# One streaming buffer for weight strips in place of two, a ninth kept strip, and the opening's strips in the ring

## The reference, cut to what matters

```
for layer in range(2):
    h = h + mixer[layer](rms_norm(h, ln_mix[layer]), weights)
    h = h + peer_ffn(rms_norm(h, ln_ffn[layer]), w_q, keys, u, v)

# peer_ffn, for a block of 128 tokens
q = (xb @ w_q)                       # 8 heads of 128
s1, s2 = q[:64] . keys[0], q[64:] . keys[1]     # 128 scores each
e, g = best 16 of the sums of (top 16 of s1) x (top 16 of s2), softmax
a = gelu(u[e] . xb) * g              # u: 16384 x 1024
out = sum over the 128 picks of a * v[e]        # v: 16384 x 1024
```

## Time and profile before

| | |
|---|---|
| median of 3 runs | 2955.15 us (2951.78 to 2957.01) |
| the profiled execution's own time | 2956.67 us |
| its span | 2954.9 us |
| PE, DVE, ACT, POOL busy | 77%, 74%, 40%, 44% |
| moved by DMA | 1176.45 MB, mean 398 GB/s |

### The profile page before, as it was taken

The page is one execution under the profiler, slowest core; times in us unless marked ns, Lnnn a source line. Parts: engine busy times, 40 slices in busy tenths (PEclk is TensorE's granted clock), DMA queues, the critical chain, the costliest instruction groups (busy, mean ns, idle before and its releaser), DMA issues.

```text
span 2954.9 us, 27833 instructions
## 1 busy us (share of the span) xinstructions
PE 2285.7 (77%) x7308; PEld 1210.5 (41%) x7308; DVE 2185.8 (74%) x5158; ACT 1182.8 (40%) x3443; POOL 1298.0 (44%) x1186
## 2 busy tenths in 40 slices
PE   8678887787877877786887878877788777886667
PEld 6535553354423544242443445433443434432222
DVE  2497778775878767796787876988779776787664
ACT  2144434343443443445344453434534444333333
POOL 0144335453345433444434544444534554255565
PEclk9789899899898989998988988988889998888889
DMA  5499999999999999999999999999999999999998
GB/s 209 170 408 421 406 416 414 421 421 406 403 419 421 421 411 420 401 422 421 415 375 398 421 421 417 367 408 421 422 386 393 404 415 412 381 406 422 422 421 364
DMA packets 164316, 1176.45 MB, mean 398 GB/s; under 512 B 18944, under 2 KB 19200, under 8 KB 22352
## 3 DMA queue, kind: packets, MB, share of 16 engines
q0 software_dynamic: 147456, 1073.81, 88.2%
q1 hardware_dynamic: 16720, 101.03, 8.5%
HBM read 1170.57 MB, written 4.19 MB: 398 GB/s over the span
## 4 chain that ended last, share of the span: by engine, by line
DMA 29%; DVE 16%; PE 15%; issue 8%; ACT 4%; POOL 4%; POOLq 0%; DVEq 0%; ACTq 0%; SPq 0%
DMA ring<-in_uv,pick_now 28%; PE acc L1608 10%; DVE ring L1060 5%; POOL ring L646 4%; PE ps L1408 3%; DVE side L1053 1%; DMA xc<-h 1%; ACT diag L1327 1%; PE ps L1397 1%; DVE arena L939 1%; DVE arena L920 1%; ACT coef L1317 1%; DVE arena L1010 1%; DVE arena L1014 1%; DVE arena L921 1%
## 5 line engine op out<-in xcount | busy, mean ns | idle before, releaser
L1608 PE MATMUL acc<-ring,diag 128*128 128x512 f32 x2988 | 1560.0, 666 | 527.8 <-ACT diag L1327 526.6
L646 POOL DMA_INDIRECT ring<-in_uv,pick_now x1024 | 1238.5, 1209 | 1509.3 <-PE acc L1608 995.3
L1060 DVE CUSTOM_DVE_ANT_0 ring<-ring,h_now 128x1024 f32<-128x1024 f32 x1024 | 1237.3, 1223 | 559.5 <-DMA ring<-in_uv,pick_now 547.9
L1608 PEld LDWEIGHTS acc<-ring,diag 128*128 128x128 f32 x2988 | 589.3, 209 | 1368.0 <-ACT diag L1327 781.8
L1314 ACT ACTIVATE gelu<-dots 128x1 f32<-128x1 f32 x1024 | 206.1, 201 | 1322.1 <-DVE dots L1060 1320.6
L1053 DVE SCALAR_TENSOR_TENSOR side<-ring,coef,side 128x1024 f32<-128x1024 f32 x270 | 345.9, 1281 | 23.5 <-ACT coef L1317 23.5
L1327 ACT ACTIVATE diag<-ident,coef 128x128 f32<-128x128 f32 x747 | 300.0, 402 | 41.0 <-PE acc L1608 16.6
L1317 ACT ACTIVATE coef<-gate,gelu 128x1 f32<-128x1 f32 x1024 | 301.4, 294 | 33.2
L1408 PE MATMUL ps<-resident,actT 128*128 128x256 f32 x768 | 184.9, 397 | 0.0
L1408 PEld LDWEIGHTS ps<-resident,actT 128*128 128x128 f32 x768 | 149.7, 198 | 37.6 <-issue 17.5
L1408 PE MATMUL ps<-stream,actT 128*128 128x256 f32 x576 | 140.7, 403 | 6.2 <-DMA stream<-in_strips 5.5
(11 more groups left out here) (189 smaller groups left out, 1387.0 us busy)
## 6 DMA issues: line engine op xcount, KB each, us to landing
stream<-in_strips SPq DMA_DIRECT2D x68, 1024.0 KB, 9.2
resident<-in_strips SPq DMA_DIRECT2D x16, 1024.0 KB, 10.7
ring<-in_uv,pick_now POOLq DMA_INDIRECT x1024, 12.7
arena<-in_keys SPq DMA_DIRECT2D x8, 512.0 KB, 12.5
xc<-in_x SPq DMA_DIRECT2D x4, 512.0 KB, 6.0
h<-arena SPq DMA_DIRECT2D x4, 512.0 KB, 11.2
xc<-h SPq DMA_DIRECT2D x4, 512.0 KB, 7.8
out<-arena SPq DMA_DIRECT2D x4, 512.0 KB, 9.3
```

The source lines that it names most:

```text
L646: pool.indirect_dma_start(ring[:, i, :], None, tables[layer], bass.IndirectOffsetOnAxis(ap=pick_now[:, half, i:i + 1], axis=0),).then_inc( ...
L1060: dve.tensor_tensor_reduce(ring[:, i, 0:D], ring[:, i, 0:D], h_now[:], 1.0, 0.0, ALU.mult, ALU.add, dots[:, i:i + 1]).then_inc(dotted, 1)
L1608: m = pe.matmul(acc[:, b * 512:(b + 1) * 512], diag[:, i % 4, :], ring[:, i, D + b * 512:D + (b + 1) * 512], start=(r == 0 and i == tensor ...
```

## The change

- `RESIDENT` is 9. Layer 0 streams 11 strips a block (r1 to r3, out0 to out3, pq0 to pq3), layer 1 streams 4 (pq0 to pq3). `STREAMED` follows.
- `stream` is one buffer `[128, 8, 256]`. The load of a streamed strip is issued when PE has used the strip just before it. (The code can cut a strip into `CUTS` parts with a semaphore each; `CUTS` is 1, so a strip is undivided.)
- In the opening, strips 9 to 16 (r1 to r3, out0 to out3, pq0) are loaded into the eight slots of `ring`, which no gather uses yet, one after the other and with no wait between them. Only pq1 to pq3 go through `stream` there.
- The keys are issued on PE's event `y` (the end of out3) ahead of pq0 in layer 0, and ahead of pq1 in layer 1.
- The pq matmuls write the two halves of a strip to two PSUM banks (2 and 3), at a column that alternates with j, where they wrote one bank (2 + j % 2). ACT's copy reads accordingly; sizes are the same.
- In `AT`, six pieces of PE in "gla" and "first" and a few in "swa" move by one to three beats, which spaces the streamed strips apart.

```diff
-RESIDENT = 8
+RESIDENT = 9
+CUTS = 1
+CUT = 8 // CUTS
-FREED = ([None, None, None, "r", None, None, None, "y", "pq0", "pq1", "pq2", "pq3"],
-         ["y", "pq0", "pq1", "pq2", "pq3"])
-GAIN_AT = (6, 2)
+DONE = ([None, None, "r", None, None, None, "y", "pq0", "pq1", "pq2", "pq3"],
+        ["pq0", "pq1", "pq2", "pq3"])
+FREED = [[e for event in events for e in [None] * (CUTS - 1) + [event]] for events in DONE]
+GAIN_AT = (4, 1)
-KEYS_AT = tuple(f.index("y") + 2 for f in FREED)
+KEYS_AT = (DONE[0].index("y") + 1, 1)
...
 AT = {
     "gla": {
-               "r0": 56, "r1": 56, "r2": 62, "upd": 62, "r3": 62, "o0": 64, "o1": 64, "oT": 69, "out0": 71,
-               "out1": 71, "out2": 76, "out3": 78, "h2T": 84, "pq0": 84, "sc0": 86, "pq1": 88, "sc1": 90, "pq2": 94,
+               "r0": 56, "r1": 56, "r2": 60, "upd": 62, "r3": 62, "o0": 64, "o1": 64, "oT": 69, "out0": 71,
+               "out1": 73, "out2": 76, "out3": 79, "h2T": 84, "pq0": 84, "sc0": 86, "pq1": 88, "sc1": 90, "pq2": 94,
...
-        stream = sb("stream", [P, 2, KT, STRIP])
+        stream = sb("stream", [P, KT, STRIP])
...
+        def in_ring(prep, n):
+            return prep.first and prep.layer == 0 and RESIDENT <= n < RESIDENT + SLOTS
...
+                opening = prep.first and prep.layer == 0
+                if opening:
+                    for n in range(SLOTS):
+                        sp.dma_start(ring[:, n, :], strips[0][RESIDENT + n]).then_inc(ring_loaded[n], 16)
                 for n in range(STREAMED[prep.layer]):
...
-                    if n >= 2:
-                        freed(prep, n - 2)
-                    elif not (prep.first and prep.layer == 0):
-                        last = STREAMED[before(prep).layer] - 1
-                        freed(before(prep), last if last % 2 == n else last - 1)
-                    sp.dma_start(stream[:, n % 2].rearrange("p k c -> p (k c)"),
-                                 strips[prep.layer][RESIDENT + n]).then_inc(slot_loaded[n % 2], 16)
                     if n == KEYS_AT[prep.layer]:
+                        said_by(sp, "pe", prep, "y")
                         sp.dma_start(keysT, (keys0, keys1)[prep.layer]).then_inc(keys_loaded, 16)
+                    for c in range(CUTS):
+                        if opening and n < SLOTS:
+                            break
+                        if n > (SLOTS if opening else 0):
+                            freed(prep, (n - 1) * CUTS + c)
+                        elif not opening:
+                            freed(before(prep), (STREAMED[before(prep).layer] - 1) * CUTS + c)
+                        sp.dma_start(stream[:, c * CUT:(c + 1) * CUT, :].rearrange("p k c -> p (k c)"),
+                                     strips[prep.layer][RESIDENT + n, :, c * CUT * STRIP:(c + 1) * CUT * STRIP])\
+                          .then_inc(slot_loaded[c], 16)
```

More of the change, by code:

```diff
@@ L205, in slot_uses @@
     def slot_uses(self, n):
-        slot = n % 2
-        per = [(STREAMED[l] + 1 - slot) // 2 for l in (0, 1)]
-        return self.p * per[self.layer] + (n // 2 + 1 + (0 if self.layer == 0 else BLOCKS * per[0]))
+        return self.p * STREAMED[self.layer] + (n + 1 + (0 if self.layer == 0 else BLOCKS * STREAMED[0])) - SLOTS
 def alone(eng, passed):
@@ L316, in build @@
         res_loaded = [sem(f"res_loaded{i}") for i in range(RESIDENT)]
-        slot_loaded = [sem(f"slot_loaded{i}") for i in range(2)]
+        slot_loaded = [sem(f"slot_loaded{c}") for c in range(CUTS)]
+        ring_loaded = [sem(f"ring_loaded{i}") for i in range(SLOTS)]
         strip_used = sem("strip_used")
@@ L412, in weight @@
                 return resident[:, n]
-            return stream[:, (n - RESIDENT) % 2]
+            if in_ring(prep, n):
+                return ring[:, n - RESIDENT, :].rearrange("p (k c) -> p k c", k=KT)
+            return stream
         def out0(prep):
@@ L1267, in turn_out @@
                     said_by(act, "pe", prep, f"pq{j}")
-                    say(act.activation(pqT[:, PART * j:PART * (j + 1), :], ps[:, 2 + j % 2, 0:PART * P].rearrange(
-                        "p (h t) -> p h t", h=PART), ACT.Copy))
+                    say(act.activation(pqT[:, PART * j:PART * (j + 1), :], ps[:, 2:4, (j % 2) * P:(j % 2 + 1) * P],
+                                       ACT.Copy))
                 upto = late_from(prep)[1]
@@ L1383, in strip, with cut_loaded, cut_done @@
             def strip(prep, n):
[L1385 to L1389, removed]
-                return weight(prep, n)
+                if n < RESIDENT and prep.first:
+                    pe.wait_ge(res_loaded[n], 16 * (prep.layer + 1))
+                return weight(prep, n)
+            def cut_loaded(prep, n, c):
+                if in_ring(prep, n):
+                    pe.wait_ge(ring_loaded[n - RESIDENT], 16)
+                elif n >= RESIDENT:
+                    pe.wait_ge(slot_loaded[c], prep.slot_uses(n - RESIDENT) * 16)
+            def cut_done(n, c, ins):
+                if n >= RESIDENT and c < CUTS - 1:
+                    used_up(ins)
             def left(prep, n, bank, side):
@@ L1400, in left, with query @@
                 return i
+            def query(prep, j):
+                n = pq0(prep) + j
+                w = strip(prep, n)
+                for cut in range(CUTS):
+                    cut_loaded(prep, n, cut)
+                    for c in range(2):
+                        for k in range(cut * CUT, (cut + 1) * CUT):
+                            i = pe.matmul(ps[:, 2 + c, (j % 2) * P:(j % 2 + 1) * P], w[:, k, c * P:(c + 1) * P],
+                                          actT[:, k, :], start=(k == 0), stop=(k == KT - 1))
+                    cut_done(n, cut, i)
+                return i
             def right(prep, n, dst, bias=None):
@@ L1407, in right @@
                 for k in range(KT):
+                    if k % CUT == 0:
+                        cut_loaded(prep, n, k // CUT)
                     i = pe.matmul(dst, actT[:, k, :], w[:, k, :], start=(k == 0 and bias is None),
                                   stop=(k == KT - 1))
+                    if k % CUT == CUT - 1:
+                        cut_done(n, k // CUT, i)
                 return i
@@ L1455, in gla @@
                     i = right(prep, 8 + n, two_banks(2, 3)[:, n * STRIP:(n + 1) * STRIP])
-                    if n < 3:
+                    if 8 + n >= RESIDENT and n < 3:
                         used_up(i)
@@ L1578, in select @@
                         said_by(pe, "act", prep, "h2T")
-                    say(left(prep, pq0(prep) + j, 2 + j % 2, 0))
+                    say(query(prep, j))
                     yield at[f"sc{j}"]
```

## The result

The changed kernel takes 2963.64 us (median of 13 runs, 2958.32 to 2970.34); the kernel before, in as many runs of the same comparison, 2955.15. The ratio is 1.0029, with a 95% interval of 1.0021 to 1.0037: slower by 0.29%, 8.5 us, where I had forecast 6.4 us less. The profiled execution has a span of 2959.5 us, 4.6 us more than the span before.

The account below looks back on a forecast made before the run. The kernel was taken as bound by DMA bytes at a 421 GB/s ceiling, plus DMA's idle time. Terms -3.2 + 2.5 - 13.5 + 10.3 - 2.5 = -6.4 us gave 2950.3, or 2948.8 as median; range 2933 to 2971.

Parts of the forecast that it names:

- the second rival: Out0 to out3, stages 0 to 2: PE's strip waits starve the ring of gathers; 12.9 us each, 2972 us, chance 0.28.
- the gla stages with pq3's slide: Stages 0 to 2: one strip less each, against r and out waits, +10.3; pq3's load hidden in stage 1's picks, -2.5.
- the swa stages: Stages 3 to 6: picks start earlier, -17.5 us, less 1 us a stage for pq1's wait; -13.5.
- the opening with pq3's load: Opening: waits of r2 and out2 go, -3.2 us; pq3's load comes after the gathers begin, +2.5.
- I take 5.0, nearer to the 6.8 that the rows leave: Out strips, stages 0 to 2: cost of PE's waits per gla stage, 5.0 us, bounds 0 and 14.9.
- the 14.9 worked out: Out1 to out3 in each gla stage: PE's waits of 5.6, 5.6 and 3.7 us together.
- The ring as a cushion: Out strips, gla stages: queued gathers let DMA go on while PE is late; one gather landed 17.68 us after issue.
- 0, at most 3: Opening: pq2 and pq3 wait 4.8 us each on PE, which has nothing to serve yet; cost 0, at most 3 us.
- three beats and the state update between r2 and r3: Stage 0, r strips: work standing between r2 and r3, so their wait costs 0, at most 1.4 us.
- The banks and tables: The pq matmuls' PSUM banks and ACT's copy were put at 0, with no change in count or size.
- The first rival: Bytes win: the ring covers the out strips' waits; 2930 us at the limit, 2940 with small waits left; chance 0.24.
- saved strips do nothing: Gla and swa: saved strips fell in time lost anyway, and swa picks start no earlier; 2955 us, chance 0.10.

Follow-up runs that it names:

- e10_late_out: e2_mixed with the changed PE tables and the loads of out1 to out3 issued late in blocks 1 to 3 of layer 0; 2956.49 us.
- e11_late_pq: e2_mixed with the loads of pq1 to pq3 issued late in blocks 1 to 3 of layer 0, keys on y; 2940.06 us.
- e9_slide: Kernel before, two buffers and all bytes, but in layer 1 keys on y and pq1 to pq3 each issued when the strip before is used; 2948.62 us.
- e2_mixed: Kernel before with e1_open's opening; layer 0 keeps eight strips and two buffers, layer 1 keeps nine and streams through one; 2929.11 us.
- e1_open: Kernel before with only the opening's strips 8 to 15 loaded into the empty ring, pq0 to pq3 through the two buffers; 2952.3 us.
- e12_reload: e2_mixed with the ninth kept strip, out3, loaded again in blocks 1 to 3 of layer 1; 2936.45 us.
- e8_bytes: e2_mixed with the load of r0's strip cut to its first eighth in blocks 1 to 3 of layer 0; 2925.4 us.

## Why the prediction was wrong

Right: what bounds the kernel, the value of a strip, the number of bytes, that the opening and the picks gain, that the out strips are the place to fear, and the mechanism of the second rival, with its place and its test: it names the starved ring, and windows far under 350 GB/s between out0 and pq0 are what it asked for. Its price, 12.9 us in each gla stage, was not right either: 16.5 in stage 0 and about 6 in the others. Wrong was the weight between that rival and the forecast. In the pieces of the sum, the gla stages with pq3's slide were put at +7.8 and are +34.0, the swa stages at -13.5 and are -26.0, the opening with pq3's load at -0.7 and is -4.7. The misses are of opposite sign: that the total is off by 15 us only, and inside the stated range, is luck.

- **The step that failed** is "I take 5.0, nearer to the 6.8 that the rows leave". The waits for out1 to out3 came to 11.8 us in stage 0 (8.52 and 3.27, none for out3) and 10.7 in stage 1 (6.21, 1.60 and 2.87), less than the 14.9 worked out, but the out strips alone cost 24 to 27 us in three stages [e10_late_out], where 15 were forecast. The cost is not even: from out0 to pq0 the changed kernel loses 16.5, 6.0 and 5.6 us. In stages 1 and 2 the 5.0 was about right; in stage 0 it was less than a third. The term was worked out from stage 1's rows and then used "in each stage", though in stage 0 one beat of PE's work stands between out0 and out1 and not two. Behind the waits came what no term had: pq0's own wait of 5.94 us, where idle time ahead of pq0 had been counted on as a cushion, and strips that took 6.19 and 5.38 us in place of 3.6. The ring as a cushion was read from a gather issued at 716.30, 17.68 us on its way. It is the last of four that POOL issued from 712.56 on, when PE's four beats in a row had freed their slots, and those four beats are what the change takes apart. A cushion must be read where the new wait starts, and there, at 692 to 700, the ring had just been empty.
- **A term left out**: the pq waits of layer 0. I priced pq3's slide as a gain of 2.5 us, and named the wait between pq0 and pq1 only in a rival. With keys and pq0 both issued on y, pq0 waited 5.94 us in stage 0, and pq1 to pq3 alone cost 11 us [e11_late_pq]. It is a gain in layer 1 only [e9_slide]. In the opening, where pq2 and pq3 were put at "0, at most 3", PE waited 3.77 and 8.48 us for them; nothing shows that these cost time, since PE began its first beat at 148.99 us, and before at 154.43.
- **r2 and r3**: "three beats and the state update between r2 and r3" did not cover r3 in stage 0, it waited 2.21 us, and r2, for which the prediction has no term there, waited 7.49: one beat of PE's work (1.88 us) stood ahead of it. I had counted beats as if they took the pace of the gathers. But up to out0 the three stages came to -1.1 us, where -4.7 was forecast (three strips' bytes and twice 1.4, where 681.8 less 680.48 is 1.3). So this miss is small.
- **Layer 1** was too small: -13.5 forecast, with -17.5 as the bound; -26.0 in the trace, and e2_mixed is 23.2 us below e1_open in the medians. Of that, 7.3 are bytes [e12_reload] and 6.7 the slid loads [e9_slide]; the other 9 stay open. Read from stages 3 to 6 of the traces instead, the bytes are 12.4 us and the slid loads 11.0, which leaves 1.6 of the 25.0 by which e2_mixed is below e1_open there. Chance is several us in either reading, so it isn't settled whether something is missing or a strip ahead of the picks costs 3 to 4 us and not 2.49. The mechanism held: in stage 4 the picks begin 258.3 us into the stage and not 265.3, 7.0 us earlier where 5.0 was forecast, and the stage is 7.0 us shorter. PE waited for one pq strip in each of the four stages, 2.6 to 3.2 us and not up to 6.
- **The opening** was -3.2 with +2.5 given back: -4.7 in the trace. The out strips gave 1.5 us, near the 1.65 that was taken; up to the turning of the attention's result PE was 2.7 us earlier (77.75 for 80.43) and not 1.59, 0.8 of it already when r0 began (48.24 for 49.06). Why is open. e1_open's gain in the median is 1.5 us, with an interval that allows 5, so how much of this reaches the whole time is open too.
- **The banks and tables** at 0: the tables are 3.7 us in the medians (interval 0 to 5 us); the banks were not run alone.
- The first rival's gain came true in layer 1, and its condition, that the ring covers the out strips' waits, failed in layer 0. That saved strips do nothing is refuted for layer 1 by e12_reload; for layer 0 e8_bytes leaves it open.

## What to carry to other kernels

A second buffer is worth what stands still while the load is on its way, so price it place by place: in this kernel three query strips issued late cost 11 us in one layer and gain 7 in the other. A term worked out in one stage holds for the next only if the same work stands between the strips there. Before an in-order engine is made to wait, look at the state of the queue that it feeds at that very place, in 4 to 8 us windows, and not at the longest transfer nearby. When one half of a change gains and the other loses, give each layer its own layout of the same memory: that is the 2929 us kernel.

## What the runs showed that I had not expected

- A wait of PE can cost more than itself. After waits of 6.21 and 8.52 us the out strip took 6.19 us where it takes 3.7, and the granted clock of that window is 0.63 (728 to 736 us), a mean between the levels 1.2 and 2.4 GHz; after waits of 1.60 and 2.87 us it took 3.69. The length of the wait alone doesn't decide: r3 of stage 0 took 5.41 us after a wait of 2.21. That adds up to 2.5 us to a strip, which no term of mine had.
- Of three ways to cut a strip the middle one was best: undivided 2963.6, halves 2940.0, quarters 2977.1 us. Quarters that were issued together came 3.1 us apart.
- A load's way is a gauge of the traffic: 9.48 us among gathers and 4.87 us a moment later, when POOL had issued nothing for 12.6 us.
